# Moving VectorE's block transposes and sums ahead of three other steps in the projection loop of a two-layer attention block

## The reference

```python
def trunk_layer(x, xt, ...):
    h = modulate(rms_norm(x, g_attn), sh_a, sc_a)
    ht = modulate(rms_norm(xt, g_attn), tsh_a, tsc_a)
    q_w, k_w, v_w, q_n, k_n, v_n, q_g, k_g, v_g = split_mixer_inputs(h @ w_in, qk_g)
    ...
    q_w, k_w = apply_rope(q_w, cos, sin), apply_rope(k_w, cos, sin)
    q_g, k_g = apply_rope(q_g, cos, sin), apply_rope(k_g, cos, sin)
    o = jnp.concatenate([window_attention(...), neighbourhood_attention(...),
                         global_block_attention(...)], axis=-1)
    x = x + ga_a * (o @ w_out)
    x = x + ga_f * swiglu(modulate(rms_norm(x, g_ffn), sh_f, sc_f), w_gate, w_up, w_down)
```

## Time and profile before

| what | value |
| --- | --- |
| median of 3 runs | 1698.17 us (1697.66 to 1699.02) |
| the profiled execution | 1697.3 us, its span 1695.5 us |
| PE busy | 1612.7 us, 95% of the span |
| DVE busy | 1063.6 us, 63% |
| ACT busy | 741.8 us, 44% |
| POOL busy | 741.5 us, 44% |
| chain that ended last | PE 66%, DVE 17%, issue 5%, DMA 4%, ACT 4%, SPq 2% |

### The profile page before, as it was taken

One profiled execution on the slowest core, in us unless ns is written; L12 is line 12 of the kernel. 1 busy time (PEld: TensorE's weight loads), 2 busy tenths in 40 slices (PEclk: granted clock), 3 DMA queues, 4 the chain that ended last, 5 costly groups with the idle time before them and its releaser, 6 DMA issues.

```text
span 1695.5 us, 29317 instructions
## 1 busy us (share of the span) xinstructions
PE 1612.7 (95%) x11471; PEld 1092.0 (64%) x11471; DVE 1063.6 (63%) x2120; ACT 741.8 (44%) x1345; POOL 741.5 (44%) x474
## 2 busy tenths in 40 slices
PE   7999989989999999999999999898999899999998
PEld 3688788878756656666666657686887544444444
DVE  4556698884488963887359756568995526227234
ACT  4222378873253431435213323226894455355342
POOL 1244345562523543435424243550403567567553
PEclk9999999999999999999999999999999999999999
DMA  9366553323226331362336222654104253253232
GB/s 321 63 148 151 128 140 87 94 70 81 63 79 183 112 100 51 107 195 84 112 104 198 88 60 61 148 123 111 29 2 108 54 137 100 63 137 100 63 96 78
DMA packets 318051, 179.22 MB, mean 106 GB/s; under 512 B 89526, under 2 KB 311258, under 8 KB 317914
## 3 DMA queue, kind: packets, MB, share of 16 engines
q1 hardware_dynamic: 285306, 143.63, 32.4%
q10 hardware_dynamic: 32608, 33.71, 6.4%
HBM read 158.97 MB, written 2.83 MB: 95 GB/s over the span
## 4 chain that ended last, share of the span: by engine, by line
PE 66%; DVE 17%; issue 5%; DMA 4%; ACT 4%; SPq 2%; ACTq 1%; POOL 1%; DVEq 0%; POOLq 0%
PE acc L973 55%; DVE mod_acc L2185 4%; DVE prob L1967 2%; DVE prob_t L1973 2%; PE small L920 2%; DMA q_sin<-q_n 1%; PE side L1159 1%; PE side L910 1%; ACTq L1458 1%; ACT prob_t L1532 1%; SPq L609 1%; DVE act L1775 1%; DVE mod_acc L2183 1%; PE acc L1142 1%; DVE scaled_ffn L1791 1%
## 5 line engine op out<-in xcount | busy, mean ns | idle before, releaser
L973 PE MATMUL acc<-act,pair_w 128*128 128x512 f16 x3168 | 579.6, 345 | 6.2 <-ACT act L1410 3.5
L973 PEld LDWEIGHTS acc<-act,pair_w 128*128 128x128 f16 x3168 | 308.9, 98 | 266.1 <-issue 10.0
L973 PE MATMUL acc<-act,split_w 128*128 128x512 f32 (+1 forms) x1920 | 379.5, 355 | 9.7 <-DVE act L2117 4.6
L973 PEld LDWEIGHTS acc<-act,split_w 128*128 128x128 f32 x1920 | 307.9, 189 | 69.2 <-DVE act L2117 6.8
L814 POOL TENSOR_SCALAR pair_raw<-pair_raw,weight_scale 128x1024 f32<-128x1024 f32 x88 | 109.5, 1244 | 325.0 <-ACT pair_w L1582 325.0
L973 PE MATMUL acc<-hidden,down_w 128*128 128x512 f16 (+1 forms) x1056 | 247.7, 343 | 1.7 <-DVE hidden L2151 0.8
L738 POOL TENSOR_SCALAR split_w<-raw_w 128x1024 fp32r<-128x1024 f32 x72 | 77.3, 1074 | 331.0 <-PE acc L973 226.1
L2185 DVE SCALAR_TENSOR_TENSOR mod_acc<-mod_chunk,silu_c,mod_acc 128x256 f32<-128x256 f32 x280 | 196.6, 745 | 4.0
L817 POOL TENSOR_TENSOR pair_w<-pair_raw,pair_w 128x1024 f16<-128x1024 f32 x88 | 192.5, 2187 | 7.3
L741 POOL TENSOR_TENSOR split_w<-raw_w,split_w 128x1024 fp32r<-128x1024 f32 x72 | 173.6, 2411 | 6.0
L2146 DVE SCALAR_TENSOR_TENSOR prod<-acc,prod_scale,silu_g 128x768 f32<-128x768 f32 (+1 forms) x44 | 38.9, 885 | 207.6 <-PE acc L973 198.6
(11 more groups left out here) (236 smaller groups left out, 2445.1 us busy)
## 6 DMA issues: line engine op xcount, KB each, us to landing
mod_chunk<-in_w_mod ACTq DMA_DIRECT2D x28, 1024.0 KB, 5.4
pair_raw<-in_w_gate SPq DMA_DIRECT2D x44, 512.0 KB, 4.0
pair_raw<-in_w_up SPq DMA_DIRECT2D x44, 512.0 KB, 5.4
raw_w<-in_w_in SPq DMA_DIRECT2D x64, 256.0 KB, 3.7
raw_w<-in_w_mod SPq DMA_DIRECT2D x24, 512.0 KB, 4.1
raw_w<-in_w_down SPq DMA_DIRECT2D x20, 512.0 KB, 4.2
mod_start<-in_w_mod SPq DMA_DIRECT2D x8, 1024.0 KB, 12.2
ks<-q_split SPq DMA_DIRECT2D x64, 96.0 KB, 2.3
```

The lines of the kernel that those rows point to most:

```text
L973: mm = pe.matmul(acc[slot][:, a:b], own, moving[:, part == 1, k, a:b], start=(k == 0 and part == 0), stop=(k == n - 1 and part == 1))
```

## The change

One call moves up within VectorE's iteration. Nothing is added or removed, and no wait changes.

```diff
                     inverse(m - 2)
+                    sum_blocks(m - 1)
                     take_values(m - 2)
                     rotate(m - 4)
                     round_low(m - 5)
-                    sum_blocks(m - 1)
                     norm_tile(m - 3)
```

## The result

The changed kernel took 1709.53 us (median; 1705.11 to 1711.87), the kernel before 1698.60 us (1697.63 to 1700.21) beside it. The ratio is 1.0066, with a 95% interval of 1.0054 to 1.0077: about 11 us slower, where 1700.8 us had been forecast, a difference counted as no change. The profiled execution took 1710.55 us (span 1708.8), against 1697.3 (1695.5).

The account below looks back on a forecast made before the run. Layer 1 was taken as bound by SyncE's queue from tile 9's low half to tile 13's norm. Layer 1's 2.7 and layer 0's 0 on 1697.3 gave 1700.0, with 0.9 for the median 1700.8 us; range 1695.8 to 1703.5.

Parts of the forecast that it names:

- Layer 1, tile 9: Layer 1's projection: root of tile 9 can run at 1109.7 to 1110.5, before 1110.82; broadcast for tile 9 slightly early.
- I take 0.6: Layer 1: swap and low halves of tile 7, stacking of tile 6, broadcast for tile 9 taken as 0.6 us early.
- depends on a DMA, not on TensorE; I leave it: Layer 0: the square of tile 12 was left ending at 175.95 us, unmoved by the change.
- at worst 0.8 later: Layer 1: the square of tile 9 ends at 1105.68 us, or at most 0.8 us after that.
- slower: Rival, 0.17: SyncE's queue passes late low halves of tiles 2 and 3 to tile 9's norm; +5.3 us, 1703.5 us.
- the signs that were to show the forecast right: Sum waits 4 to 5 us; waits for values at tile 12; layer 1's tile 9 stacking 2 to 3 us later.
- Layer 1, tiles 4, 6 and 7: Layer 1: tile 4's wait gone; tile 6's follow-up 3.4 us ahead, tile 7's 2.9 after waiting about 4 us.
- Layer 1, tile 12 and 13: Layer 1: values and sums delay the low half of tile 9 by 2.7 us, passed on to the norm of tile 13.
- Layer 0: Layer 0's projection: a wait for values replaces that for sums at tile 12; gain 0, bounds -1.5 and +0.5 us.
- 10 us of cover for norm 13: Layer 0: SyncE's slack was to absorb a low half of tile 9 that is 4.7 us late.
- The first rival: Both layers: all 9.8 us of TensorE's waits for sums are won, giving 1688.4 us; chance 0.12.
- before they had run while ScalarE issued the swaps and squared: Layer 1, tile 12: tile 11's values, 3.06 us, now follow the sums and end at 1136.8 instead of 1133.21.

Follow-up runs that it names:

- e8: Kernel before with the sums moved ahead of values, rotation and low half at every tile but 6 and 7, both layers: 1700.31 us, 1.0010.
- L V S R: Kernel before with VectorE's four calls in the order low half, values, sums, rotation: 1690.15 us, 0.9956.
- e11: Kernel before with VectorE's calls reordered to low half, values, sums, rotation: 1690.15 us, 0.9956 of the kernel before.
- e3: Kernel before with the sums moved ahead of values, rotation and low half at tiles 6 and 7 alone, both layers: 1706.35 us, 1.0050.
- e17: Changed kernel with the values put ahead of the sums at tile 6 only: 1701.49 us, 1.0025 of the kernel before.
- e13: Kernel before with the sums moved ahead of values, rotation and low half at tile 6 alone: 1705.87 us, 1.0047.
- e1: Kernel before with the sums moved ahead of values, rotation and low half in layer 0 alone: 1702.38 us, 1.0032.

## Why the prediction was wrong

The step that failed is "Layer 1, tile 9", with its end "I take 0.6", and the sentence for layer 0 that the square of tile 12 "depends on a DMA, not on TensorE; I leave it". Norm 9 was to start 0.6 us early in layer 1 and unmoved in layer 0; it came 1.4 us late in the one (1133.88 less the shift of 5.26, against 1127.20) and 2.9 late in the other (175.48 less 1.88, against 170.71). The first term that fails is the square of tile 9, "at worst 0.8 later": it was 2.2 us late in layer 1, because norm 6 was 3.0 us late, and norm 6 stands in no line of my own sum. I had the delay of norm 4 right (0.7 forecast, 0.9 measured) but followed it only to the next sums, not along the low halves into SyncE's queue. The rival "slower" named this road, the stack of tile 3 and then the broadcasts, and its point of decision, the start of norm 9. I gave it 0.17 and worked it out for 1 us of lateness, which is near the 1.4 of layer 1 and far below the 2.9 of layer 0. Its ground against, later waits that would swallow the delay, held only in part: norm 6 was 4.9 and 3.0 us late in the two layers, and norm 9 still 2.9 and 1.4. Of the signs that were to show the forecast right, the waits for sums were to fall to 4 or 5 us (measured 1.7 and 8.4, as much as before), and the stacking of tile 9 in layer 1 to come 2 to 3 us later (6.6). TensorE's wait for the values at tile 12 came in both layers (3.63 us, and 1.25 in layer 1, where it ends as the values do).

*Layer 1, tiles 4, 6 and 7.* Right: the wait at tile 4 is gone, at tile 6 it is 1.02 us, and tile 7's is 3.97, as the 4 us said. Less the shift the follow-ups of tiles 6 and 7 ran at 1081.3 and 1091.4, forecast at 1081.2 and 1091.3. The wait for sums at tile 9 (1.74 us), which made four of three, was not forecast; TensorE's lead of 2.8 us at tile 7 was 1.0 behind it.

*Layer 1, tile 12 and 13.* Right in mechanism, sized too small: low half 9 is 6.65 us late, not 2.7. The difference closes with two numbers: norm 9 is 2.0 us later than taken (1.4 late for 0.6 early), and the rotation of tile 9 took 2.77 us on line 1930, not 0.69: 2.7 + 2.0 + 2.1 = 6.8. The road from there to norm 13 ran as forecast (6.97 us late), though the idle in front of it, forecast at 3.5 us, is 2.07: VectorE's own work there is late as well. That the closing is this good is in part luck, since the 2.1 us are a meeting with GpSimd that stood in no term (last section). The road over norm 12 to TensorE's wait of 3.6 us on line 1078 stood in none either.

*Layer 0.* The wait for values came, as said, and its 10 us of cover for norm 13 held (5.7 us late there, no more than the first score, though low half 9 was 7.9 late and not 4.7). But the sum of 0 was wrong: 3.63 us of waiting, ended 3.27 later than the follow-up in before (186.32 less 181.17 less 1.88), and 2.36 us of slow dense tile: 5.6, where 5.73 is the whole loss of this projection. That the wait would be followed by a lower clock stood in no term. (The terms of the forecast add up to 1700.9 us, not 1700.8; nothing hangs on it.)

*The first rival* came from the rule of the Trainium skill to issue a DMA early, compute, and wait late ("DMA: Bandwidth & Descriptors", section "Rules for kernel authors"). The rival failed: the waits for sums in layer 1 were 8.4 us, not 0. The move had put VectorE's wait of 4 us ahead of ready computation, not behind it. *That VectorE's cover is used up by the values* stood in my text as "before they had run while ScalarE issued the swaps and squared"; I priced it at tile 12 alone, and at tile 6 had the values only delay norm 4. The runs show the same cover at tile 6 (7.0 us) as at tile 12 (6.3 us).

What stays open: the parts don't add up. The sums ahead of everything at all tiles but 6 and 7, with tile 12 among them, lose only 1 to 1.7 us, while tile 12's values are worth 6.3 in the changed kernel. That tile 12 is dear only when norm 9 is late would explain layer 0 (0.43 us of wait there in e8). For layer 1 the trace of e8 shows norm 9 and low half 9:

```profile
1124.74 0.75 DVE L1884 SCALAR_TENSOR_TENSOR q_n<-raw_q,vecs,root 128x512 f32<-128x512 f32 x1 [1.85 <-DMA root<-inv_rows]
...
1141.95 0.68 DVE L1917 TENSOR_TENSOR q_split<-q_raw,q_split 128x512 f16<-128x512 f32 x1
```

Less its first follow-up (0.32 earlier than in before), norm 9 is 2.1 us early, low half 9 is 2.6 late and norm 13 2.7 late. These are the 2.7 us that I had forecast for the changed kernel, though from a norm 9 that is 2.1 early and not 0.6, and with a meeting with GpSimd on the way (low half 8 at 1137.09 took 2.66 us for 0.69). From norm 9 to low half 9 the move at tile 12 costs 4.7 us there and 5.2 in the changed kernel (1.4 late to 6.6 late). So tile 12's cost and the lateness of norm 9 add up at low half 9, and in e8 an early norm 9 pays for nearly half of the cost. How much of this reaches the end of the kernel stays open.

## What to carry to other kernels

In an in-order queue, rank calls by when their inputs are ready, not by who waits for their result: a step whose input is late must not stand ahead of ready work that would fit into its wait. Here that was 1.9 and 3.3 us of work in waits of 4.1 and 4.3 us, and worth 13 us. Follow each step that becomes late into every queue that waits for it, the DMA issuer's above all, and through what is queued behind it there, until a slack is measured that swallows it. If only one step of a loop must come sooner, try first to move ahead of it what is ready and what another queue waits for: here L V S R beat the two kernels by 7.5 and 19 us (0.9956 against 1 and 1.0066).

## What the runs showed of the hardware

In these traces a VectorE operation with two inputs in SBUF stands still while a pass of GpSimd that began before it runs. Low half 3 of the changed kernel (137.05, 2.94 us for 0.96) and rotation 9 (1144.58, 2.77 for 0.69) meet these rows of GpSimd:

```profile
136.45 2.73 POOL L741 TENSOR_TENSOR split_w<-raw_w,split_w 128x1024 fp32r<-128x1024 f32 x1
...
1144.09 2.71 POOL L741 TENSOR_TENSOR split_w<-raw_w,split_w 128x1024 fp32r<-128x1024 f32 x1
```

The first ends at 139.18 and the low half 0.81 later; the second at 1146.80 and the rotation 0.55 later, so nearly the whole operation runs after GpSimd's. The one-input pass of line 738 does the same (135.32, 1.05 us): rotation 4 at 135.40 took 1.50 us for 0.69. In e11 the one-input transpose of VectorE at 1132.58 lay within a pass of line 741 (1131.90 for 2.71) and took 0.98 us as ever. The Trainium skill, "Trainium Architecture — The Big Picture", section "What this means for kernel authors", calls the ports that VectorE and GpSimd share "an exclusive lock (not a bandwidth split)"; the trace agrees. So a delay can grow by 2 us just by where it lands (2.94 less 0.96, 2.77 less 0.69).

TensorE's clock: in the rows below (e3, layer 0, follow-up of tile 9) as in the changed kernel, a wait of some 4 us that begins at the full clock is followed by a dense tile that takes 1.3 to 2.4 us longer than 8.73.

```profile
157.26 0.38 PE L1070 MATMUL mod_ps<-by_head,block_sums 128*24 128x64 f32 x2 [4.49 <-DVE block_sums L1860]
157.57 10.07 PE L973 MATMUL acc<-act,split_w 128*128 128x512 f32 x48
```

Waits of 3.63 and 3.67 us had 11.09 and 10.26 behind them, waits of 1.50 (e17) and 1.74 us (layer 1 of the changed kernel, tile 9) the usual 8.73. A wait of 6.78 us (e13, tile 7) had 10.76 behind it. In e1 the clock was still at 1.00 through the whole wait of 3.67 us and at its lower level only as the tile began (0.53 from 184.9 to 187 us); in the changed kernel it fell within the wait. So the surcharge isn't in proportion to the wait, and in the sum of a prediction such a wait stands for more than its length.
